# Taking the light expert's raw down chunks between the heavy expert's gate and up chunks, in loads and in matmuls

## The reference, cut to what matters

```python
logits = (ht @ w_router + b_router).astype(jnp.float32)
top_vals, top_idx = lax.top_k(logits, TOP_K)
gates = jax.nn.softmax(top_vals, axis=-1)
...
gu = xblk @ w_gate_up[e] + b_gate_up[e]
gate = jnp.minimum(gu[:, :D_EXPERT], SWIGLU_LIMIT)
up = jnp.clip(gu[:, D_EXPERT:], -SWIGLU_LIMIT, SWIGLU_LIMIT)
act = gate * jax.nn.sigmoid(SWIGLU_ALPHA * gate) * (up + 1)
return act @ w_down[e] + b_down[e]
```

## Time and profile before

| What | Value |
|---|---|
| Median of 3 runs | 1778.67 us (1777.46 to 1783.34) |
| Profiled execution, its own time | 1780.13 us |
| Its span, first to last instruction | 1778.5 us |
| TensorE busy | 1611.2 us (91%) |
| VectorE busy | 1068.7 us (60%) |
| ScalarE busy | 781.4 us (44%) |
| Moved by DMA | 496.42 MB |

### The profile page before, as it was taken

One profiled execution on the slowest core, in us unless ns is written; L12 is line 12 of the kernel. 1 busy time (PEld: TensorE's weight loads), 2 busy tenths in 40 slices (PEclk: granted clock), 3 DMA queues, 4 the chain that ended last, 5 costly groups with the idle time before them and its releaser, 6 DMA issues. The chain is left out here.

```text
span 1778.5 us, 22633 instructions
## 1 busy us (share of the span) xinstructions
PE 1611.2 (91%) x7599; PEld 1089.3 (61%) x7600; DVE 1068.7 (60%) x1418; ACT 781.4 (44%) x996; POOL 265.9 (15%) x348
## 2 busy tenths in 40 slices
PE   6998987999899899899899899899899899998998
PEld 3555455646646656656655645556565468878996
DVE  5466755635635645645645645645588567987663
ACT  5443312533533533533533533534563654436541
POOL 0140321010010010010010010010064000005420
PEclk9997968999999999999999999999999899999999
DMA  6031836999999999999999999999998412201001
GB/s 219 8 117 65 338 139 225 412 393 389 421 395 392 420 393 395 421 396 398 408 394 398 414 393 379 404 394 381 417 387 294 147 62 93 95 25 72 1 25 48
DMA packets 107661, 496.42 MB, mean 279 GB/s; under 512 B 22817, under 2 KB 40846, under 8 KB 57330
## 3 DMA queue, kind: packets, MB, share of 16 engines
q1 hardware_dynamic: 97554, 474.02, 67.0%
q0 software_dynamic: 10048, 21.64, 3.7%
HBM read 476.60 MB, written 19.02 MB: 279 GB/s over the span
## 5 line engine op out<-in xcount | busy, mean ns | idle before, releaser
L2023 DVE TENSOR_TENSOR part<-ring,part 128x2048 fp32r<-128x2048 f32 x138 | 314.6, 2295 | 120.9 <-ACT part L1579 120.7
L1579 ACT ACTIVATE part<-ring 128x2048 fp32r<-128x2048 f32 x136 | 256.8, 1913 | 209.8 <-DMA ring<-in_w_down 174.1
L1823 PE MATMUL bank<-part,actT_hi 128*128 128x512 f32 x544 | 166.9, 433 | 56.1 <-DVE part L2023 55.8
L1767 PE MATMUL bank<-part,xT_hi 128*128 128x512 f32 x816 | 207.3, 396 | 0.0
L2023 DVE TENSOR_TENSOR part<-rest,part 128x2048 fp32r<-128x2048 f32 x64 | 146.0, 2303 | 66.3 <-ACT part L1579 66.3
L1767 PEld LDWEIGHTS bank<-part,xT_hi 128*128 128x128 f32 x816 | 149.7, 188 | 33.0 <-issue 3.9
L1823 PEld LDWEIGHTS bank<-part,actT_hi 128*128 128x128 f32 x544 | 114.5, 214 | 85.6 <-DVE part L2023 52.9
L1795 PE MATMUL bank<-ring,rest 128*64 128x512 f32 x720 | 163.7, 595 | 2.1 <-ACT rest L1599 1.4
L1579 ACT ACTIVATE part<-rest 128x2048 fp32r<-128x2048 f32 x64 | 120.8, 1912 | 21.6 <-DMA rest<-in_w_down 19.6
L1795 PEld LDWEIGHTS bank<-ring,rest 128*64 128x64 f32 x720 | 49.8, 137 | 99.1 <-issue 87.5
L2227 POOL DMA_INDIRECT rest<-h_rows,rest x17 | 17.3, 1019 | 619.2 <-PE bank L1743 582.5
(11 more groups left out here) (554 smaller groups left out, 2817.6 us busy)
## 6 DMA issues: line engine op xcount, KB each, us to landing
ring<-in_w_gate_up SPq DMA_DIRECT2D x194, 1024.0 KB, 9.2
ring<-in_w_down SPq DMA_DIRECT2D x66, 1024.0 KB, 9.2
rest<-in_w_gate_up SPq DMA_DIRECT2D x62, 1024.0 KB, 9.6
rest<-in_w_down SPq DMA_DIRECT2D x62, 1024.0 KB, 9.7
ring<-in_w_in SPq DMA_DIRECT2D x14, 1024.0 KB, 5.1
rest<-in_w_ada SPq DMA_DIRECT2D x8, 1536.0 KB, 6.7
ring<-in_w_out SPq DMA_DIRECT2D x16, 512.0 KB, 6.0
expert_rows<-rest SPq DMA_DIRECT2D x16, 512.0 KB, 7.9
```

Source lines behind the costliest of these rows:

```text
L1579: nc.scalar.activation(hi[part], raw_slot(m, slot), ACT.Copy).then_inc(sig("hi_ready"), counts)
L1767: ins = nc.tensor.matmul(bank[g][:], rows[:, c, :], w[:, g * 512:(g + 1) * 512], start=first, stop=last, skip_group_check=True)
L1823: ins = nc.tensor.matmul(bank[6 + g][:], rows[:, n, :], w[:, k, g * 512:(g + 1) * 512], start=first, stop=last, skip_group_check=True)
L2023: V.tensor_tensor(lo[part], raw_slot(m, slot), hi[part].bitcast(F32), ALU.subtract).then_inc(sig("lo_ready"), counts)
```

## The change

In the big turn the order of the chunks becomes 0, 1, 2, 8, 9, 3, 4, 5, 6, 10, 7, 11 (`BIG_TURN`), in loads, in slots (position in the order modulo 6) and on TensorE: raw downs 8 and 9 stand behind gate-up chunk 2, down 10 behind chunk 6, down 11 behind chunk 7. Both row lists are made in the big turn (the light expert's behind chunk 2, the heavy one's at the end), in bank 7; the heavy rows' transposes stand between downs 9 and 10 of the small turn. ScalarE and VectorE take their work in an order to suit: VectorE does the light expert's clip and products right behind the first `lo`, ScalarE copies the heavy rows behind `hi` 5 and the light activations behind `hi` 8. GpSimd loads biases ahead of the gather. SP issues the stores of `y` one or two loads later.

```diff
+    SMALL_TURN = (0, 1, 2, 3, 4, 5, 6, 7, 8, 9, 10, 11)
+    BIG_TURN = (0, 1, 2, 8, 9, 3, 4, 5, 6, 10, 7, 11)
...
+            def wait_big(j, n):
+                c = BIG_TURN[n]
+                if c < 8:
+                    wait_lo(sp, first(j) + 4 + c)
+                else:
+                    wait_raw(sp, j, c)
+
+            def rest_of_small(j, e, before, store=True):
+                for n in range(SLOTS, CHUNKS):
+                    wait_small(j, n - SLOTS)
+                    load_nth(SMALL_TURN, n, e, before)
+                    if n == 6 and store:
+                        store_small(j - 1)
...
             def rest_of_big(j, e, before):
-                for c in range(SLOTS, CHUNKS):
-                    wait_lo(sp, first(j) + 4 + c - SLOTS)
-                    load_chunk(sp, a, m, e if c < 8 else before, c, c % SLOTS)
+                for n in range(SLOTS, CHUNKS):
+                    wait_big(j, n - SLOTS)
+                    load_nth(BIG_TURN, n, e, before)
+                    if n == 7:
                         store_big(j)
...
+            def after_big(j, turn, e, before):
+                for n in range(SLOTS):
+                    wait_big(j, n + SLOTS)
+                    load_nth(turn, n, e, before)
...
+                pool.wait_ge(sig("rows_turned"), 2 * j + 2)
+                load_biases(e)
                 gather(2 * j + 2)
...
-            def small_turn(j):
+            def pair(j):
 
                 nc.scalar.activation(spare[0:1, 0:1], con(m, "ident", 1)[0:1], ACT.Sigmoid)
                 copy_act(j + 1)
                 hi_of_pair(j, 0)
                 hi_of_pair(j, 1)
                 sigmoid_small(j)
-                hi_of_pair(j, 2)
-                hi_of_pair(j, 3)
+                for s in (2, 3, 4, 5):
+                    hi_of_pair(j, s)
                 copy_rows(2 * j + 2, j + 2)
-                hi_of_pair(j, 4)
-                hi_of_pair(j, 5)
+                hi_of_pair(j, 6)
                 copy_y(first(j) + 3, 32 * j + 32, "y_small_stored")
-                hi_of_pair(j, 6)
                 hi_of_pair(j, 7)
+                hi_of_pair(j, 8)
                 copy_act_small(j)
+                for s in (9, 10, 11):
+                    hi_of_pair(j, s)
...
                 first_small(j)
+                next_small(j, 2)
                 turn_act(0, j + 1)
                 turn_act(1, j + 1)
...
+                small_down(j, 8)
+                small_down(j, 9)
                 turn_rows(i + 1)
-                pe.wait_ge(sig("index_ready"), i + 3)
-                for c in range(8, CHUNKS):
-                    down(first(j) + c - 8, c - 8, c)
+                small_down(j, 10)
+                small_down(j, 11)
...
+            def big_turn(j, more=True):
 
                 i = 2 * j + 2
                 pe.wait_ge(sig("clipped_small"), j + 1)
                 first_gate_ups(first(j) + 4, (4, 5), j + 2, [("act_small", j + 1)])
                 turn_act_small()
+                big_gate_up(j, 2)
+                pe.wait_ge(sig("y_ready"), i + 1)
+                list_next(i + 1)
+                pe.wait_ge(sig("actT_small"), j + 1)
+                down_small(j, 8)
+                down_small(j, 9)
+                for c in (3, 4, 5, 6):
+                    big_gate_up(j, c)
+                down_small(j, 10)
                 biases(i)
+                big_gate_up(j, 7)
+                down_small(j, 11)
                 if more:
+                    list_next(i + 2)
+                    turn_rows_small(i + 1)
+                else:
+                    turn_rows(i + 1)
...
+                lo_of_pair(j, 0)
+                clip_small(j)
+                gated_small(j)
+                times_gate_small(j)
+                for s in (1, 2, 3, 4, 5):
+                    lo_of_pair(j, s)
+                rows_lo(j + 2)
+                lo_of_pair(j, 6)
+                lo_of_pair(j, 7)
```

More of the change, by code:

```diff
@@ L1382, in experts, with slot_of @@
     LAST, FINAL = CHUNKS * (PAIRS + 1), CHUNKS * (PAIRS + 2)
+    SMALL_TURN = (0, 1, 2, 3, 4, 5, 6, 7, 8, 9, 10, 11)
+    BIG_TURN = (0, 1, 2, 8, 9, 3, 4, 5, 6, 10, 7, 11)
+    PLAIN_TURN = tuple(range(CHUNKS))
+    def slot_of(turn, c):
+        return turn.index(c) % SLOTS
     def first(j):
@@ L1439, in after_small, with load_nth @@
[L1439 to L1456, removed]
-                        store_big(j)
+            def load_nth(turn, n, e, before):
+                c = turn[n]
+                load_chunk(sp, a, m, e if c < 8 else before, c, n % SLOTS)
@@ new lines, in rest_of_big, with after_small @@
+            def rest_of_big(j, e, before):
+                for n in range(SLOTS, CHUNKS):
+                    wait_big(j, n - SLOTS)
+                    load_nth(BIG_TURN, n, e, before)
+                    if n == 7:
+                        store_big(j)
+            def after_small(j, e, before):
+                for n in range(SLOTS):
+                    wait_small(j, n + SLOTS)
+                    load_nth(BIG_TURN, n, e, before)
+            def after_big(j, turn, e, before):
+                for n in range(SLOTS):
+                    wait_big(j, n + SLOTS)
+                    load_nth(turn, n, e, before)
@@ L1459, in _ @@
             e_small = expert_at(sp, 1)
-            for c in range(RAW):
-                wait_lo(sp, c + 8 - RAW)
-                load_chunk(sp, a, m, e_small, c, c)
+            for n in range(RAW):
+                wait_lo(sp, n + 8 - RAW)
+                load_nth(SMALL_TURN, n, e_small, 0)
             sp.wait_ge(sig("x_stored"), 16 * T)
[L1464 to L1467, removed]
+            for n in range(RAW, SLOTS):
+                load_nth(SMALL_TURN, n, e_small, 0)
@@ L1468, in _ @@
+            rest_of_small(0, e_small, 0, store=False)
+            after_small(0, expert_at(sp, 2), e_small)
             with sp.Fori(0, PAIRS - 1) as j:
@@ L1581, in hi_of_pair @@
             def hi_of_pair(j, s):
-                c = s + 8 if s < 4 else s - 4
-                make_hi(s % PARTS, c % SLOTS, f"chunk_loaded{c}", 2 * j + 1 if s < 4 else 2 * j + 3, first(j) + s - PARTS)
+                c, turn = (s + 8, SMALL_TURN) if s < 4 else (s - 4, BIG_TURN)
+                make_hi(s % PARTS, slot_of(turn, c), f"chunk_loaded{c}", 2 * j + 1 if s < 4 else 2 * j + 3, first(j) + s - PARTS)
             def hi_of_last(c, counts=1):
@@ L1659, in _ @@
             with act.Fori(0, PAIRS - 1) as j:
-                small_turn(j)
-                for s in range(8, CHUNKS):
-                    hi_of_pair(j, s)
+                pair(j)
                 sigmoid(first(j) + 11)
@@ L2092, in act_lo, with pair @@
                 V.tensor_tensor(flat(actT_lo, h), bank[4 + h][:], flat(actT_hi, h).bitcast(F32), ALU.subtract).then_inc(sig(f"actT_lo{h}"), 1)
-            def small_turn(j, last=False):
+            def pair(j, last=False):
                 at = 2 * j + 3
@@ L2102, in small_turn @@
                 act_lo(1, j + 1)
+                lo_of_pair(j, 0)
[7 more added lines that the diff above has]
+                lo_of_pair(j, 7)
                 if last:
[L2104 removed]
+                    index(at, 7)
                 else:
[L2106 to L2114 removed]
+                    index_small(at, 7)
+                lo_of_pair(j, 8)
+                if not last:
+                    list_of(iota, expert_at(dve, at + 1))
+                for s in (9, 10, 11):
+                    lo_of_pair(j, s)
             list_of(iota_small, expert_at(dve, 1))
[L2117 removed]
+            index_small(1, 3)
             rows_lo(1)
@@ L2129, in _ @@
             with dve.Fori(0, PAIRS - 1) as j:
-                small_turn(j)
-                list_of(iota, expert_at(dve, 2 * j + 4))
-                for s in (6, 7, 8, 9, 10):
-                    lo_of_pair(j, s)
-                index(2 * j + 4)
-                lo_of_pair(j, 11)
+                pair(j)
                 clip(first(j) + 11)
@@ L2138, in _ @@
                 times_gate(j + 1)
+                index(2 * j + 4, 7)
             j = PAIRS - 1
-            small_turn(j, last=True)
-            for s in range(6, CHUNKS):
-                lo_of_pair(j, s)
+            pair(j, last=True)
             clip(first(j) + 11)
```

107 lines of the change are left out of this document (42 added, 65 removed).

## The result

The changed kernel takes **1796.31 us** in the median of 4 runs (1794.93 to 1797.66), the kernel before 1778.75 beside it: ratio 1.0087, 95% interval 1.0068 to 1.0106. It is slower; the forecast was 1763, faster, and even its range ended at 1785. The profiled execution took 1796.78 us.

The account below looks back on a forecast made before the run. Neither DMA nor TensorE alone but a loop of two legs: 46.6 + 2.9 + 15.5 = 65.0, plus 0.6 clock, 65.6 us a pair. From 1780.13, -19 + 4 gives 1765, median 1763; 8-in-10 range 1741 to 1785.

Parts of the forecast that it names:

- TensorE's leg: From first split down to release of raw chunks 0 and 1: 46.6 us of work, 2.9 of waits, 0.6 for the clock.
- the wait of 1.6 for the second `lo`: At the split downs, VectorE's clip and two products delay the second `lo`, so TensorE waits 1.6 us.
- The wait of 0.7 for the light rows' copy: At the turn's end, the copy behind the light rows' transposes is no longer covered by raw downs: 0.7 us with signals.
- The wait for the light activations' copy: Before raw down 8, TensorE may wait for the copy behind `hi` 8 on ScalarE: 0.6 us, between 0 and 2.5.
- DMA's leg: From release of raw chunks 0 and 1 to the next first split down: 15.1 us summed, 0.4 added, 15.5.
- The heavy gather: Bias loads delay GpSimd's gather about 2 us; rows are wanted some 20 us after its start, so cost 0.
- SP's moves: Stores move behind later loads; SP waits at most for the copy while the queue holds several loads: 0.
- the 8 us without issues: SP's issue gap at the pair's seam, waiting for raw down 8's slot, goes as raw downs move forward.
- nothing left: Rival, chance 0.14: queue drains 1 us each mid-turn, at down 8 and at the seam; pair 66.7 us, kernel 1779 us.
- The rival at 1793: Slower by the clock, chance 0.14: low clock after waits before the downs goes on into gate-ups; pair 67.7 us.
- Cost of the end: In the last pair, less TensorE work covers ScalarE and VectorE before the last expert's gate-ups: 3.4 to 5.2 us, taken as 4.
- The start: The first pair starts from full slots: cost 0.

Follow-up runs that it names:

- chunk 0 first: Changed kernel, but TensorE takes all four matmuls of the light expert's chunk 0 before those of chunk 1: 1789.6 us, ratio 1.0064.
- two faster kernels: Changed kernel with light activations copied ahead of `hi` 8, without and with later light stores; moving the heavy gather later took them from 1791.9 to 1773.5, 1774.5 to 1764.2 us.
- the stores moved back: Light expert's two stores behind the small turn's tenth load, not seventh, in kernels with light activations copied ahead of `hi` 8: 1764.2 us with heavy gather later, 1774.5 without.
- the kernel with three edits: Changed kernel with heavy gather later, light activations copied ahead of `hi` 8, chunk 0's matmuls before chunk 1's: 1771.7 us; with four unused matmuls ahead of the downs, 1770.9.
- two edits beside it: Changed kernel with the heavy gather behind the light expert's last gate-up chunk and light activations copied ahead of `hi` 8: 1773.5 us, ratio 0.9966.
- the plain order: Heavy turn's chunks back to 0 to 11, here against the kernel with three edits: 1766.9 us; against the changed kernel alone: 1796.8 us.
- late gather: Changed kernel, but GpSimd gathers the heavy expert's rows only once the light expert's last raw gate-up chunk is used: 1789.9 us, ratio 1.0063.
- early copy: Changed kernel, but ScalarE copies the light expert's activations ahead of `hi` 8 instead of behind it: 1791.9 us, ratio 1.0056.
- one surrounding: Heavy turn in the plain order against the kernel with late gather, early copy and light stores behind the tenth load: 1779.8 us for 1764.2.
- two others: Heavy turn in the plain order against the changed kernel, 1796.8 us for 1796.3, and against the kernel with three edits, 1766.9 for 1771.7.

## Why the prediction was wrong

**The bound.** Right in the main: neither TensorE nor DMA alone is it in the changed kernel, and a pair is two legs in series. But the legs aren't independent: with chunk 0 first, 1.3 of the 1.9 us that came off one came back on the other.

**TensorE's leg.** 50.1 forecast, 50.5 measured. Inside it two terms were wrong and cancelled: the wait of 1.6 for the second `lo` didn't come, since the low clock filled it, and the downs take longer by the clock (14.31 us from first down to first gate-ups in the mean, not 10.9 + 1.0 + 1.6 + 0.6 = 14.1). The wait of 0.7 for the light rows' copy came as 0.87. The wait for the light activations' copy was put at 0.6 between bounds of 0 and 2.5; it was 0.1, and 1.3 as soon as the gather was late.

**DMA's leg: the step that failed.** "The heavy gather starts about 4 us into the pair and its rows are wanted behind down 9, some 20 us later: 0." The start was right enough (779.91, 2.4 us behind the pair's first raw matmuls at 777.55); the cover was looked for on the wrong side. I asked when the rows are wanted, not which transfers stand behind the gather's 0.52 MB: chunks 6, 7 and 8, the three in the sum of DMA's leg. That sum has the 0.25 MB of the light expert's results and not the gather. The leg measured 17.25 for 15.5, and 15.73 with the gather moved; on two faster kernels the same move took 0.9 and 1.8 us off it (16.7 to 15.8, 16.2 to 14.4). The transfers were counted on SP's queue and not on GpSimd's, whose bytes the page counts against the same 16 engines.

A second term of this leg was put at nothing, that of SP's moves, since the queue was to hold several loads meanwhile. The sum has the stores' bytes, but not the 1.20 us that SP takes to issue them between the light chunks 6 and 7, at the place where the queue runs dry. Chunk 7 was asked for 2.1 us behind chunk 6 in the mean, and 0.6 with the stores moved back; that was worth 9 us of 1773.5 and 17 of 1791.9. On the changed kernel by itself it wasn't run.

**The gaps.** "Moving the raw downs forward frees their slots in turn, so the 8 us without issues go": half right. The gap at the seam shrank to 5.2 us; one of 8.8 opened behind raw down 8. It was foreseen in the rival *nothing left*, with 1 us dry in each of three places and 3.0 in all; measured are 4.2 in two. That rival had the mechanism, and with 1779 for 1796 too small a size.

**The clock.** The rival at 1793 came out nearest in time, by luck and with the wrong mechanism. Its condition didn't come: behind 812.56 the gate-ups run at full clock (eight in 1.98 us, not 3.58 as in the earlier trace rows), and the granted clock is 1.00 at the first gate-ups of all 15 pairs. The downs did start at 0.50 to 0.62 in all 15 pairs, as the rule of the Trainium skill cited ahead says (page "TensorE: Matmul & The Clock Gate", section "HAM oscillation — how this bites in real kernels"); restoring 1.00 there bought nothing in the kernel with three edits, where waits for `lo` took its place; the changed kernel itself wasn't run so.

**The end and the start.** Cost of the end 4 forecast, 4.0 measured (74.06 to 78.10); the wait of some 4 us at the last expert's first gate-ups is 4.30:

```profile
1322.78 3.53 PE L1802 MATMUL bank<-part,xT_hi 128*128 128x512 f32 x8 [4.30 <-DVE part L2045]
```

The start: 0 forecast, 0.1 measured. Left over are 1.6 us behind 1350.10 that no step had; over all kernels here that stretch takes 443.4 to 446.1.

**The sum.** 14 x (67.74 - 65.6) = 30 of the 33 us between forecast and result lie in the period, and 25 of these in the DMA leg (1.75 x 14). Part of the forecast gain could be had with the change's order, by two edits beside it: 1773.5 us is 5 below the kernel before, where 16 were forecast. The order isn't shown to be its source: in the plain order, with chunk 0 first, the kernel takes 1766.9 for 1771.7.

**What stays open.** Why the kernel before is faster than the changed one, with the gather at the seam in both, beyond what the stores and the 4 us of the end may account for: late gather and early copy on the kernel before, and later stores alone on the changed one, were not run. How much of the early copy's 0.3% alone is real, and why the plain order suffers so much more in one surrounding (1.05 us a pair) than in two others (none).

## What to carry to other kernels

When a step is moved, ask of each of its transfers what will now be queued behind it on the DMA engines, not only when its own data is wanted; here a gather on another engine's queue took about its bytes' time from the loads on the critical chain, and two small stores the time of their issue. Where one wait comes out as soon as another is removed, remove both before judging either: here each alone was worth a quarter to a third of a per cent, and together 1.2. And add up a pair in bytes at full rate plus dry time; a gap in the issues that closes in one place is worth something only if none opens in another.

## What was not expected of the hardware

A gather of 128 rows of 4 KB from GpSimd, issued 1.5 us ahead of a 1 MB load on SP's queue, lengthened the way from that load to the downs by 1.5 us, and by 0.9 and 1.8 in two other kernels; its bytes take 1.25 at 421 GB/s. And a granted clock of 0.50 to 0.68 over the first 4 us of a 14 us stretch, seen in 12 of 15 pairs, cost nothing that could be measured while the operands came from a DMA stream at 406 GB/s.
